# Spreading the gate rows of an mLSTM over 128 partitions: selector products on TensorE, or a broadcast through DRAM

## The reference

```python
def step(carry, chunk):
    c, n, m = carry
    qc, kc, vc, ic, lfc = chunk
    b = jnp.cumsum(lfc, axis=-1)
    inter = b + m[..., None]
    intra = jnp.where(mask, b[..., :, None] - b[..., None, :] + ic[..., None, :], -jnp.inf)
    m_t = jnp.maximum(inter, jnp.max(intra, axis=-1))
    w_inter = jnp.exp(inter - m_t)
    s = jnp.einsum('bhtd,bhsd->bhts', qc, kc) * jnp.exp(intra - m_t[..., None])
    num = w_inter[..., None] * jnp.einsum('bhvk,bhtk->bhtv', c, qc) + jnp.einsum('bhts,bhsv->bhtv', s, vc)
    den = w_inter * jnp.einsum('bhk,bhtk->bht', n, qc) + jnp.sum(s, axis=-1)
    h = num / jnp.maximum(jnp.abs(den), jnp.exp(-m_t))[..., None]
```

## Time and profile before

| | |
|---|---|
| median of three runs | 1524.04 us (1517.58 to 1527.65) |
| profiled execution, device time | 1523.02 us |
| its span in the profile | 1521.4 us |
| busy share of the span | PE 93%, PEld 89%, DVE 55%, ACT 34%, POOL 7% |
| mean granted PE clock | 0.957 of full speed |
| transfers | 167.86 MB, mean 110 GB/s |

### The profile page before, as it was taken

How to read it: one execution, slowest core, us unless ns; L and a number is a source line. 1 busy time by engine, 2 the same in 40 slices (tenths; PEclk the granted TensorE clock), 3 DMA queues, 4 the chain that set the end, 5 groups by cost and what they waited for, 6 DMA issues and landing times.

```text
span 1521.4 us, 29729 instructions
## 1 busy us (share of the span) xinstructions
PE 1421.0 (93%) x11874; PEld 1349.3 (89%) x11874; DVE 844.3 (55%) x1277; ACT 524.2 (34%) x856; POOL 100.4 (7%) x138
## 2 busy tenths in 40 slices
PE   5999999788999999999999898997799999999997
PEld 4889899678999999999998677775699999999997
DVE  5355357564666666623253777778446666665221
ACT  4333434334333232322233454554243332322110
POOL 0021111112000000000000000000020000000000
PEclk9899999779999999999999999997799999999999
DMA  5443243212222223322126666773022222233320
GB/s 199 70 144 80 99 113 107 53 59 84 79 88 97 86 93 94 120 96 91 59 91 209 183 221 193 220 252 129 22 95 93 88 97 85 94 99 109 113 90 21
DMA packets 45820, 167.86 MB, mean 110 GB/s; under 512 B 5882, under 2 KB 7210, under 8 KB 45498
## 3 DMA queue, kind: packets, MB, share of 16 engines
q1 hardware_dynamic: 38506, 143.77, 29.0%
q0 software_dynamic: 7248, 23.15, 6.1%
HBM read 155.42 MB, written 11.48 MB: 110 GB/s over the span
## 4 chain that ended last, share of the span: by engine, by line
PE 84%; DVE 6%; issue 4%; ACT 4%; DMA 1%; POOL 0%; DVEq 0%; ACTq 0%; POOLq 0%
PE ps L516 55%; PE ps L567 13%; PE ps L696 2%; DVE mx L2084 1%; PE ps L925 1%; PE ps L1028 1%; ACT w_hi L1097 1%; ACT e_att L1455 1%; PE ps L631 1%; PE ps L879 1%; PE ps L1004 1%; PE ps L941 1%; PE ps L738 1%; PE ps L928 1%; DMA qb<-q_rows 1%
## 5 line engine op out<-in xcount | busy, mean ns | idle before, releaser
L516 PE MATMUL ps<-h_hi,w_hi 128*128 128x260 f32 x1616 | 459.4, 284 | 5.1 <-DVE h_lo L1562 4.6
L1553 DVE TENSOR_TENSOR w_lo<-raw,w_hi 128x1024 fp32r<-128x1024 f32 (+1 forms) x189 | 245.0, 1296 | 390.8 <-ACT w_hi L1097 390.8
L516 PE MATMUL ps<-h_hi,w_lo 128*128 128x260 f32 x1616 | 457.9, 283 | 0.0
L516 PE MATMUL ps<-h_lo,w_hi 128*128 128x260 f32 x1616 | 456.3, 282 | 0.0
L516 PEld LDWEIGHTS ps<-h_hi,w_hi 128*128 128x128 f32 x1616 | 305.4, 189 | 6.9 <-issue 4.4
L516 PEld LDWEIGHTS ps<-h_lo,w_hi 128*128 128x128 f32 x1616 | 305.2, 189 | 0.2
L516 PEld LDWEIGHTS ps<-h_hi,w_lo 128*128 128x128 f32 x1616 | 305.2, 189 | 0.0
L1097 ACT CAST w_hi<-raw 128x1024 fp32r<-128x1024 f32 (+1 forms) x189 | 208.0, 1101 | 224.3 <-PE ps L516 216.7
L516 PE MATMUL ps<-a_lo,w_hi 128*128 128x260 f32 x704 | 199.0, 283 | 0.0
L516 PE MATMUL ps<-a_hi,w_hi 128*128 128x260 f32 x704 | 198.8, 282 | 0.0
L516 PE MATMUL ps<-a_hi,w_lo 128*128 128x260 f32 x704 | 198.8, 282 | 0.0
(11 more groups left out here) (381 smaller groups left out, 2121.6 us busy)
## 6 DMA issues: line engine op xcount, KB each, us to landing
raw<-in_w_ffn SPq DMA_DIRECT2D x88, 512.0 KB, 3.4
raw<-in_w_down SPq DMA_DIRECT2D x32, 704.0 KB, 4.1
k_pages<-in_cache_k SPq DMA_DIRECT2D x32, 512.0 KB, 4.3
v_pages<-in_cache_v SPq DMA_DIRECT2D x32, 512.0 KB, 6.1
raw<-in_w_rec_in SPq DMA_DIRECT2D x29, 512.0 KB, 4.9
raw<-in_w_att_kv SPq DMA_DIRECT2D x24, 512.0 KB, 4.1
raw<-in_w_rec_out SPq DMA_DIRECT2D x8, 512.0 KB, 3.7
raw<-in_w_att_q SPq DMA_DIRECT2D x8, 512.0 KB, 3.5
```

The costliest lines, as they stand in the source:

```text
L516: ins = TE.matmul(half(bank, h), w_part[:, buf, w], m_part[:, k_at + k, h * HALF:(h + 1) * HALF], start=start, stop=stop)
L1553: V.tensor_tensor(w_lo[:, n % 2, 0:nk * P], raw[:, n % RAW, 0:nk * P], w_hi[:, n % 2, 0:nk * P].bitcast(F32), ALU.subtract).then_inc(lo_sp ...
```

## The change

The selector products and their constant go. POOL writes the four gate tensors to a DRAM scratch once, waits until they have landed, and then loads each row back with a broadcast source, so that it lands on all 128 partitions of the buffer in which its exponent is computed: `r_intra` in `e_mat`, `r_inter` in `w_int`, `r_negm` in `e_negm`, and the sample numbers of all heads at once in the new buffer `r_all`. DVE's mask and ACT's exponentials then work in place in SBUF. For heads 1 to 3 the loads are issued in the head before, as soon as the buffer is free. `e_negm` gets memory of its own, and its exponential moves behind the copies of `k` and `v`. On PE the wait for the head before (`rms`) moves from ahead of the scores to ahead of the transposes. The core of the diff:

```diff
-CONSTS_REC = [("causal_T", P), ("ones_lo", P), ("ones_hi", P), ("sel_head", M_HEADS * P), ("near", (len(NEAR) + 2) * BLK),
+CONSTS_REC = [("causal_T", P), ("ones_lo", P), ("ones_hi", P), ("near", (len(NEAR) + 2) * BLK),
...
+        e_negm = place("e_negm", [P, T], at=at)
+        r_all = place("r_all", [P, M_HEADS, 3 * B], at=at)
...
                 if h == 0:
                     pe.wait_ge(drained, len(FIRST_SLABS))
-                    wait(pe, gtD, "mo0")
                     wait(pe, gtA, "acol")
                 else:
-                    wait(pe, mD, "cq", h - 1)
-                    wait(pe, mA, "rms", h - 1)
-                for bank, row in ((0, r_intra), (1, r_inter), (6, r_negm)):
-                    TE.matmul(ps[:, bank, :], SEL[0:4, h, :], row[:, :], start=True, stop=True).then_inc(mP.sem, 1)
-                TE.matmul(ps[:, 4, 0:3 * B], SEL[0:4, h, :], r_s[:, :], start=True, stop=True).then_inc(mP.sem, 1)
+                    wait(pe, mA, "abs", h - 1)
                 for c in range(NC_M):
                     t = slice(c * P, (c + 1) * P)
                     ins = TE.matmul(ps[:, 7, t], k[:, t], q[:, t], start=True, stop=True)
                 ins.then_inc(mP.sem, 1)
                 part(0)
+                if h:
+                    wait(pe, mA, "rms", h - 1)
                 for bank, rows in ((5, v), (4, k)):
-                    if bank == 4:
-                        wait(pe, mA, "ws", h)
...
                 wait(pe, mD, "p", h)
-                wait(pe, mA, "en", h)
...
-                wait(act, mP, "bcs", h)
-                S.activation(w_s[:, :, :].rearrange("p a b -> p (a b)"), ps[:, 4, 0:3 * B], ACT.Exp).then_inc(mA.sem, 1)
-                S.activation(w_int[:, :], ps[:, 1, :], ACT.Exp).then_inc(mA.sem, 1)
                 if h:
-                    wait(act, mD, "mix", h - 1)
-                S.activation(e_negm[:, :], ps[:, 6, :], ACT.Exp).then_inc(mA.sem, 1)
+                    wait(act, mD, "rd", h - 1)
+                else:
+                    act.wait_ge(s_rows_in, 16)
+                S.activation(w_s[:, :, :].rearrange("p a b -> p (a b)"), r_all[:, h, :], ACT.Exp).then_inc(mA.sem, 1)
+                act.wait_ge(inter_in, 16 * (h + 1))
+                S.activation(w_int[:, :], w_int[:, :], ACT.Exp).then_inc(mA.sem, 1)
                 wait(act, mD, "em", h)
...
                 S.copy(v_tok[:, :, :].rearrange("p c k -> p (c k)"), ps[:, 5, :]).then_inc(mA.sem, 1)
+                act.wait_ge(negm_in, 16 * (h + 1))
+                S.activation(e_negm[:, :], e_negm[:, :], ACT.Exp).then_inc(mA.sem, 1)
...
-                wait(dve, mP, "bc0", h)
-                V.tensor_tensor(e_mat[:, :, :], ps[:, 0, :].rearrange("p (c t) -> p c t", c=NC_M),
-                                cols_(c_("causal_T"), NC_M), ALU.add).then_inc(mD.sem, 1)
+                dve.wait_ge(intra_in, 16 * (h + 1))
+                V.tensor_tensor(e_mat[:, :, :], e_mat[:, :, :], cols_(c_("causal_T"), NC_M), ALU.add).then_inc(mD.sem, 1)
...
             wait(pool, gtA, "acol")
+            for n, row in enumerate((r_intra, r_inter, r_negm)):
+                pool.dma_start(a["gate_rows"][n], row[:, :]).then_inc(gates_out, 16)
+            pool.dma_start(a["gate_s"], r_s[:, :]).then_inc(gates_out, 16)
+            pool.wait_ge(gates_out, 64)
+
+            def gate_row(n, h):
+
+                to, landed_ = ((e_mat[:, :, :].rearrange("p c t -> p (c t)"), intra_in), (w_int[:, :], inter_in),
+                               (e_negm[:, :], negm_in))[n]
+                pool.dma_start(to, a["gate_rows"][n, h:h + 1, :].to_broadcast([P, T])).then_inc(landed_, 16)
+
+            for n in range(3):
+                gate_row(n, 0)
+            pool.dma_start(r_all[:, :, :], a["gate_s"].unsqueeze(0).to_broadcast([P, M_HEADS, 3 * B])).then_inc(s_rows_in, 16)
...
                 if h < M_HEADS - 1:
+                    gate_row(0, h + 1)
                     sample_rows(h + 1)
                 wait(pool, mD, "nend", h)
                 pool.dma_start(a["o_c"][:, h], c_n[:, 0:P]).then_inc(c_out, 16)
+                if h < M_HEADS - 1:
+                    wait(pool, mD, "den", h)
+                    gate_row(1, h + 1)
+                    gate_row(2, h + 1)
                 wait(pool, mD, "cs", h)
```

More of the change, by code:

```diff
@@ L192, in build @@
         hnum_s = place("hnum_s", [P, B], at=at)
+        e_negm = place("e_negm", [P, T], at=at)
+        r_all = place("r_all", [P, M_HEADS, 3 * B], at=at)
         assert at[0] <= norm_at, (at[0], norm_at)
         row_q, row_k = v_end[:, :, :, :].rearrange("p c a v -> p (c a) v"), kv[:, :, :]
-        h_head, den, e_negm = sq[:, 1, :], rstd[:, 0:T], hn[:, 0, 0:T]
+        h_head, den = sq[:, 1, :], rstd[:, 0:T]
         at = [region]
@@ L337, in build @@
         gtP = Steps(sem("gate_pe"), "acol")
-        mP = Steps(sem("mlstm_pe"), "bc0 bc1 bc2 bcs scores vtr ktr num0 st0 num1 st1 num2 st2 num3 st3 dens ssq")
-        mA = Steps(sem("mlstm_act"), "ws wi en e kt vt abs abs_s sq lr rms")
+        mP = Steps(sem("mlstm_pe"), "scores vtr ktr num0 st0 num1 st1 num2 st2 num3 st3 dens ssq")
+        mA = Steps(sem("mlstm_act"), "ws wi e kt vt en abs abs_s sq lr rms")
         mD = Steps(sem("mlstm_dve"), "em qw ve p cn0 cn1 cn2 cn3 nend den rden h vw kw nw ns nq kv cs cq hs dn rd hs2 t mix")
@@ L342, in build @@
         mG = Steps(sem("mlstm_pool"), "cw")
+        gates_out, s_rows_in = sem("gates_out"), sem("s_rows_in")
+        intra_in, inter_in, negm_in = sem("intra_in"), sem("inter_in"), sem("negm_in")
         rows_out, kb_in, qb_in = sem("rows_out"), sem("kb_in"), sem("qb_in")
@@ L610, in v_chunks @@
                 ins.then_inc(vP.sem, 1)
-            SEL = c_("sel_head").rearrange("p (h m) -> p h m", h=M_HEADS)
             for h in range(M_HEADS):
@@ L2417, in constants @@
     causal_t = np.where(before, 0, NEG).astype(f)
-    sel = np.zeros((P, M_HEADS, P), f)
-    for h in range(M_HEADS):
-        sel[h, h] = 1
     at_, to_ = i[:, None] % BLK, np.arange(BLK)[None, :]
@@ L2426, in constants @@
     rec = {"causal_T": causal_t, "ones_lo": np.tile(lo, (P, 1)), "ones_hi": np.tile(~lo, (P, 1)),
-           "sel_head": sel.reshape(P, -1), "near": np.concatenate(near, axis=1),
+           "near": np.concatenate(near, axis=1),
            "reset_m": np.tile(t % LC_M != 0, (P, 1))}
@@ L2503 @@
     aps["v_rows"] = nc.dram_tensor("v_rows", (2 * G_PAIRS, B, P), mybir.dt.float32, kind="Internal").ap()
+    aps["gate_rows"] = nc.dram_tensor("gate_rows", (3, M_HEADS, T), mybir.dt.float32, kind="Internal").ap()
+    aps["gate_s"] = nc.dram_tensor("gate_s", (M_HEADS, 3 * B), mybir.dt.float32, kind="Internal").ap()
     aps["past"] = nc.dram_tensor("past", (B, P, 2 * P), mybir.dt.float32, kind="Internal").ap()
```

## The result

The changed kernel took 1510.76 us in the median of eight runs (1508.14 to 1515.63), the kernel before 1521.49 us on the same chip: a ratio of 0.9931, 95% interval 0.9904 to 0.9957. So the gain is 0.7%, real, and within the 1% that the prediction called "no change". The profiled execution took 1510.75 us with a span of 1509.2; before it was 1523.02 and 1521.4.

A forecast was written before the change was run, and what follows sets the result against it. PE was taken to bound the kernel, with 84% of the last-ending chain and 14.64 us of selector products in it. Head gains of 0.15, 2.90, 3.90 and 6.00 us, together 12.95, took 1523.02 to 1510 us; range 1502 to 1520.

The forecast's parts named there:

- no change: Whole kernel: about 1% is what a measurement can tell from no change; chance of landing within it 0.54.
- The sum: Gains of 0.15, 2.90, 3.90 and 6.00 us in heads 0 to 3, together 12.95, giving 1510 us.
- The products removed: All four heads: the selector products' 14.64 us leave PE's order, if PE finds its next work ready.
- The clock in heads 2 and 3: The clock's fall goes: `part(0)` gains 1.50 us in head 2, 1.84 in head 3; head 3's scores gain 0.92.
- the slow clock stays: Rival: the fall is not the selector products'; heads 2 and 3 give 2.40 and 3.24, time 1514 us; chance 0.18.
- The 0.5 of `e_negm`: The moved exponential on ACT's way to `part(1)`'s drain costs 0.5 us in heads 0 and 2, nothing in 1 and 3.
- Head 0: First DMA trip, unhidden: 2.15 us of the 5.60 gained, less 0.5 for `e_negm` and 1.5 for the clock: 0.15.
- a sign that the prediction itself had named: Listed as showing the prediction wrong: in head 0 no PE idle time, or more than 8 us.
- It lands at 66.5: Head 0: `r_all`, last of four loads, issued by 62.0 and taking 4.5 us, lands at 66.5.
- my upper bound of 6.4: Head 0's last load: upper bound of 6.4 us, from `kv<-rows`, a broadcast of 512 KB; lower bound 2.3.
- The rows of heads 1 to 3 come late: Rival: `r_inter`, issued behind element-wise sample writes, lands late; at 32 us it costs 29.4 us, time 1539; chance 0.06.
- point of decision: Late-rows rival: head 1's `r_inter` landing costs time only if over 22.2 us behind its issue at 92.2.

The follow-up runs named there:

- experiment 3: Changed kernel with head 0's load of `r_all` issued behind the element-wise writes of its sample rows: 1518.58 us, ratio 0.9986 to the kernel before.
- experiment 6: Changed kernel with the sample writes of heads 1 to 3 issued behind the loads of `w_int` and `e_negm`: 1514.78 us, ratio 0.9949 to the kernel before.
- experiment 8: The changed kernel again, unedited, on another chip: 1513.54 us over 12 runs, ratio 0.9934 to the kernel before.
- experiment 7: Changed kernel with writes and two loads ahead of POOL's `a_col` wait, later heads' sample writes behind gate-row loads, `e_negm`'s exponential behind `part(1)`'s drain: 1500.64 us, ratio 0.9856.
- experiment 2: Changed kernel with `r_all` loaded first of head 0's four loads instead of last: 1508.53 us, ratio 0.9918 to the kernel before.
- experiment 4: Changed kernel with head 0's rows from four-row selector products again, heads 1 to 3 still by DMA: 1507.44 us, ratio 0.9910 to the kernel before.
- experiment 9: Changed kernel with POOL waiting until `r_all` has landed before issuing head 0's sample writes: 1509.71 us over 6 runs, ratio 0.9929 to the kernel before.
- experiment 1: Changed kernel with head 0's four scratch writes and the loads of `r_all` and `e_negm` moved ahead of POOL's wait for `a_col`: 1499.11 us, ratio 0.9862.
- experiment 5: Kernel before, with selector products contracting over 128 rows, 124 of them zero, instead of four: 1514.69 us, ratio 0.9945 to the kernel before.

## Why the prediction was right, and where it wasn't

*The sum.* 12.95 us were forecast and the span fell by 12.2. By parts it was: head 0 +0.15 forecast, -3.44 measured (with the 0.3 that lie ahead of it); heads 1 to 3 12.80 forecast, 13.62 measured; behind the mLSTM nothing forecast, 2.0 measured. The miss in head 0 was made up by the other two, so the number was better than its working. The gain of heads 1 and 3 is the same within 0.05 us in all nine traces with the rows of these heads loaded by DMA, that of head 2 is not: it took 48.2 us in the changed kernel and in experiments 3, 6 and 8, 48.3 in 7, 48.9 to 49.1 in 2, 4 and 9, and 50.9 in 1, by whether the clock fell behind the idle time of 2.1 to 2.65 us ahead of its `part(2)`.

*The products removed* (14.64 us): right in heads 1 to 3. The scores stand directly behind the last slab, and no exponential or mask of these heads waits for a transfer.

*The clock in heads 2 and 3* (1.50, 0.92 and 1.84): right in size, and its cause is now shown by experiments 4 and 5: the fall comes and goes with the four-row products (which in head 1 ran without one). The rival that the slow clock stays, the first of the list, is out. The Trainium skill, "TensorE: Matmul & The Clock Gate" (HAM oscillation — how this bites in real kernels), which lays a falling clock to idle gaps, would by the prediction's reading have kept the fall. The runs show it gone, and in experiment 4 a fall with no idle time in the window.

*The 0.5 of `e_negm`*: shown in head 2 by experiment 7. Yet head 2 gained 0.5 more than forecast, since the products behind its idle time ran at full clock this time: the first 12 took 1.71 us (174.20 to 177.20, clock 1.00) where those before took 2.97 at 0.50, though the gap ahead of them had grown. Of these 1.26 us 0.42 count; for the rest PE waits for DVE's `c_n`.

*Head 0* is the step that failed, and by a sign that the prediction itself had named: more than 8 us of idle time ahead of `part(1)`, where 3.4 were forecast and 9.4 came. "It lands at 66.5" was the term: `r_all` landed at 69.92. 1.18 us of the 3.42 lie in the issue, which my sum had at 61.45 and which was at 62.63: I gave the writes 2.0 us, and the third and fourth took 3.6 and 3.8 (1.9 and 2.2 where experiment 1 issues them earlier). The other 2.24 are the load: 4.5 and its issue of 0.55 in the sum, 7.29 measured, above my upper bound of 6.4 as well. I had sized it by its bytes and by broadcasts that stood alone; what counts is what stands ahead of it, as experiments 2, 3 and 9 show (3.7 first, 6.5 to 7.7 fourth, 12.4 behind the element-wise writes; the 15.5 of experiment 6, also fourth, is not explained by it). From the landing to `part(1)` it was 2.47 us, forecast 2.5. The loss to the clock behind the gap was 2.7, not 1.5. Against that, the 0.5 of `e_negm` wasn't paid in head 0: from the end of `part(1)` to head 1 it took 31.9 us, 0.5 less than before. The Trainium skill's rule in "DMA: Bandwidth & Descriptors" (Anatomy of one DMA — SWDGE (gpsimd) path) would, by the prediction's estimate, have had the four loads there at 64.2; that is 5.7 too early.

Not all of the added idle time is late landing. PE arrived at that gap 2.5 us earlier than I had it (63.0 for 65.55): it started 0.3 earlier, and in head 0, too, the clock was at 1.00, so the scores took 0.9 instead of 2.00 and `part(0)` 5.8 instead of 7.06. In head 0 of the kernel before the clock was at 0.50 almost from the start of the selector products on (0.51 over them), and I had not credited it. That gain went into waiting.

*The rows of heads 1 to 3 come late.* Half of this rival came true: `w_int` takes 13.8 us. But its point of decision was 22.2, and experiment 6 shows that making it early is worth nothing.

*Behind the mLSTM* 2.0 us were gained that no step names: 0.8 up to the transposes of the next layer's gate part (L777) and 1.2 from there to the end. That last stretch, the same code in all kernels, took 1228.9 us in experiment 1, 1233.8 and 1233.9 in experiments 3 and 4, 1229.5 in the changed kernel and 1230.8 before; the stretch ahead of it took 22.9 in experiment 1, 25.4 in the changed kernel, 26.2 before and 27.3 in experiment 5. So both pieces are inside what one execution differs from another. The 2.0 isn't an effect of the change that these runs could show.

## What to carry to other kernels

Before a hand-over moves from PE to DMA, split its instances into those that can be issued a stage ahead and the first one, which can't: the later ones gave all of the gain here, and the first one took a quarter of it back until its writes were issued as soon as their data existed (11 us by order alone). Price a small transfer by what stands ahead of it in its queue, not by its bytes, and give the load that is waited for first the first place. And look at the clock over short products with few rows: if it falls behind them, padding them to full rows is the cheap repair.

## What the runs showed of the hardware that I had not expected

- PE's clock fell from 2.4 to 1.2 GHz during products of four rows while PE showed no idle time (0.76 in experiment 4, 0.87 in the earlier trace rows), and stayed at 1.00 with 128 rows of which 124 are zero (experiment 5). In head 1 of the kernel before it stayed at 1.00 with four rows as well.
- An idle gap alone didn't settle the clock: behind 2.65 us it was 1.00 in head 2 of the changed kernel, behind 2.10 it was 0.50 in the kernel before. Experiment 1 had 2.63 us there, and the clock fell about 1.5 us behind them. Behind 6.8 us and more `part(1)` took 7.5 to 8.6 us in each of the six executions read.
- The same load of 48 KB landed 3.2 us (experiment 4) to 15.5 us (experiment 6) after its issue. Broadcast loads of 256 KB took 4.2 ahead of element-wise writes and 13.8 behind them.
